# A last tile in two halves ahead of each norm, and a new order of the first loads and of the last norm

## The reference

```python
for l in range(DEPTH):                                   # block one, twice
    x = x + 0.5 * swiglu_ffn(rms_norm(x, ffn1_norm[l]), ffn1_w_in[l], ffn1_w_out[l])
    h = rms_norm(x, mix_norm[l])
    ...                                                  # gMLP, latent attention, SSD; three sigmoid gates
    x = x + merged @ w_out[l]
    x = x + 0.5 * swiglu_ffn(rms_norm(x, ffn2_norm[l]), ffn2_w_in[l], ffn2_w_out[l])
for i in range(DEPTH):                                   # block two: retention, then neighbourhood attention
    h = gated_residual(h, ml, 0, swiglu(ada_in(h, norm_g[i, 0], ml, 0), ffn_w_in[i, 0], ffn_w_out[i, 0]), 0.5)
    h = gated_residual(h, ml, 1, mixer(ada_in(h, norm_g[i, 1], ml, 1)), 1.0)
    h = gated_residual(h, ml, 2, swiglu(ada_in(h, norm_g[i, 2], ml, 2), ffn_w_in[i, 1], ffn_w_out[i, 1]), 0.5)
return rms_norm_2(h, final_norm_g)

def rms_norm(x, gain):
    return x * lax.rsqrt(jnp.mean(x * x, axis=-1, keepdims=True) + EPS) * gain
```

## Time and profile before

| what | value |
|---|---|
| median of three runs | 3204.93 us (3204.53 to 3206.68) |
| time of the profiled execution | 3203.71 us |
| its span, first to last instruction | 3201.80 us |
| TensorE busy, matmuls | 3140.3 us, 98% |
| VectorE, ScalarE, GpSimd busy | 1992.3, 1357.8, 129.9 us |
| mean granted clock of TensorE | 0.997 |
| instructions | 39778 |

### The profile page before, as it was taken

One profiled execution on the slowest core, in us unless ns is written; L12 is line 12 of the kernel. 1 busy time (PEld: TensorE's weight loads), 2 busy tenths in 40 slices (PEclk: granted clock), 3 DMA queues, 4 the chain that ended last, 5 costly groups with the idle time before them and its releaser, 6 DMA issues.

```text
span 3201.8 us, 39778 instructions
## 1 busy us (share of the span) xinstructions
PE 3140.3 (98%) x15550; PEld 2619.4 (82%) x15550; DVE 1992.3 (62%) x2797; ACT 1357.8 (42%) x1907; POOL 129.9 (4%) x160
## 2 busy tenths in 40 slices
PE   8999999999999999999999999999999999999998
PEld 7888888888888887888878888788887788887787
DVE  7968778788687787663344444776335643345665
ACT  6546655455566555323233333322223322245553
POOL 1000000000000000000000000300000000021000
PEclk9999999999999999999999999999999999999999
DMA  8765356677554576542332222254324633253354
GB/s 252 250 193 178 127 197 224 223 236 242 157 184 132 197 246 207 188 147 93 105 99 80 79 93 86 99 171 156 108 92 158 212 117 105 93 139 92 106 189 153
DMA packets 334901, 496.78 MB, mean 155 GB/s; under 512 B 11042, under 2 KB 221884, under 8 KB 334716
## 3 DMA queue, kind: packets, MB, share of 16 engines
q1 hardware_dynamic: 330652, 483.46, 45.5%
q0 software_dynamic: 4064, 10.77, 1.6%
HBM read 493.09 MB, written 1.10 MB: 154 GB/s over the span
## 4 chain that ended last, share of the span: by engine, by line
PE 94%; DVE 3%; issue 1%; ACT 1%; DMA 0%; POOL 0%; SPq 0%; DVEq 0%; POOLq 0%; ACTq 0%
PE bank L587 24%; PE bank L589 23%; PE bank L588 23%; PE bank L643 13%; PE bank L647 7%; PE bank L602 1%; DVE wlo L1750 0%; PE bank L788 0%; PE bank L773 0%; PE bank L1067 0%; DMA raw<-in_w_in_dram 0%; DVE bank L2592 0%; POOL small L2660 0%; PE bank L610 0%; ACT npr L1698 0%
## 5 line engine op out<-in xcount | busy, mean ns | idle before, releaser
L1750 DVE TENSOR_TENSOR wlo<-raw,whi 128x1024 fp32r<-128x1024 f32 (+1 forms) x780 | 939.6, 1213 | 893.7 <-ACT whi L1231 891.6
L1231 ACT ACTIVATE whi<-raw 128x1024 fp32r<-128x1024 f32 (+1 forms) x780 | 815.9, 1050 | 1150.3 <-PE bank L589 990.3
L587 PE MATMUL bank<-xTh,whi 128*128 128x512 f32 (+1 forms) x1312 | 508.2, 387 | 7.2 <-DVE xTl L1835 7.2
L589 PE MATMUL bank<-xTh,wlo 128*128 128x512 f32 (+1 forms) x1312 | 504.0, 384 | 0.0
L588 PE MATMUL bank<-xTl,whi 128*128 128x512 f32 (+1 forms) x1312 | 503.7, 384 | 0.0
L643 PE MATMUL bank<-xT,whi 128*128 128x512 f32 x1760 | 441.5, 393 | 0.9 <-DVE xT L1835 0.5
L587 PE MATMUL bank<-whi,hh 128*128 128x512 f32 x968 | 377.9, 390 | 0.0
L589 PE MATMUL bank<-whi,hl 128*128 128x512 f32 x968 | 376.8, 389 | 0.0
L588 PE MATMUL bank<-wlo,hh 128*128 128x512 f32 x968 | 376.6, 389 | 0.0
L643 PEld LDWEIGHTS bank<-xT,whi 128*128 128x128 f32 x1760 | 316.5, 189 | 63.0 <-issue 3.4
L587 PEld LDWEIGHTS bank<-xTh,whi 128*128 128x128 f32 x1312 | 246.6, 188 | 66.9 <-issue 16.3
(11 more groups left out here) (383 smaller groups left out, 3651.9 us busy)
## 6 DMA issues: line engine op xcount, KB each, us to landing
raw<-in_ffn_w_in_dram SPq DMA_DIRECT2D x176, 1024.0 KB, 5.2
raw<-in_ffn_w_out_dram SPq DMA_DIRECT2D x80, 1024.0 KB, 5.1
mraw<-in_w_mod_dram SPq DMA_DIRECT2D x72, 1024.0 KB, 5.1
raw<-in_w_in_dram SPq DMA_DIRECT2D x44, 1024.0 KB, 5.2
raw<-in_ret_w_in_dram SPq DMA_DIRECT2D x24, 1024.0 KB, 5.1
raw<-in_w_branch_dram SPq DMA_DIRECT2D x12, 1024.0 KB, 5.0
raw<-in_nat_w_qkv_dram SPq DMA_DIRECT2D x12, 1024.0 KB, 5.2
raw<-in_ffn_w_out_dram SPq DMA_DIRECT2D x16, 512.0 KB, 3.4
```

What stands on the lines that cost most here:

```text
L587: pe.matmul(ps, lh, rh, start=start, stop=False, skip_group_check=True)
L589: return pe.matmul(ps, ll, rh, start=False, stop=stop, skip_group_check=True)
L1231: nc.scalar.activation(hi, src, ACT.Copy).then_inc(*e.inc("hi", key, part))
L1750: nc.vector.tensor_tensor(lo, src, hi.bitcast(F32), ALU.subtract).then_inc(*e.inc("lo", key, part))
```

## The change

Seven edits. (1) `rows_by_tile` multiplies the last tile, in the closing slabs, 256 columns at a time: the first half in the tile's own bank, the second from its first closing k on in a bank of its own; `rows` adds three pieces: first, begun (what the own bank had of the second half), rest. This holds for all norms but f1 of layer 0 and g2 of layer 1; behind retention the whole last slab is in halves, with two pieces. (2) The last tile's square of columns 512 to 767 is ScalarE's, that of 768 to 1023 VectorE's, with the sum so far as its start, straight into GpSimd's power. The scaling of the tile before stands between the first piece and the begun one. (3) g2 of layer 0: all squares on ScalarE, scalings one tile later. g2 of layer 1: tile 0 scaled by ScalarE alone. (4) Transposes: tile-by-tile groups for all norms, k by k in the second half, a new order of banks. (5) With 512 rows, half of the low part of the next slab's second part is made ahead of the last scaling. (6) Opening: X in two loads, the identity alone ahead of the slabs, the other constants behind slab 2, the seven norm loads issued by ScalarE, the eight others by GpSimd ahead of its first power; the first part's high rounding on VectorE, its low part behind the turned X, the second part's high rounding between the third and fourth of ScalarE's turned X. (7) End: X times `fg` before the power, scaled afterwards by VectorE (640 columns) and ScalarE (384), four stores.

```diff
-PAIRS, DOWNS, TURNS, MODS, PARAMS = (0, 1, 2, 3, 4, 5), (2, 3, 4, 5), (0, 1, 2, 3, 6, 7, 4, 5), (6, 7), (6, 7, 4)
+PAIRS, DOWNS, TURNS, MODS, PARAMS = (0, 1, 2, 3, 4, 5), (2, 3, 4, 5), (0, 1, 6, 7, 3, 4, 5, 2), (6, 7), (6, 7, 4)
+REST_OF = {"downs": "rest_down", "short": "rest_short", "all": "all"}
...
+def halved(name):
+    return name not in (("f1", 0), ("g2", 1))
+
+def squared_on_act(name, t):
+    return t % 2 == 1 or name == ("g2", 0)
+
+def pieces_of_rows(name, t, n, whole=False):
+    if n == 0 or t != last_tile(name) or not halved(name):
+        return [Piece(n)]
+    first = Piece(n, ("first",), (), 0, 256, True, whole)
+    begun = [] if whole else [Piece(n, ("begun",), (), 256, 256, False, True, True)]
+    return [first, *begun, Piece(n, ("rest",), ("rest",), 0, 256, after_first=whole)]
...
+    if (name, t) == (("g2", 1), 0):
+        return (("act", 0, 512), ("act", 512, 512))
...
-            sp.dma_start(X[:, 0:2, :], w["x"][0].rearrange("(t p) n -> p t n", p=P))\
-              .then_inc(L.sem("x_landed"), 16)
-            sp.dma_start(cst[:, :], consts["cst"][:, 0:C_FLIP]).then_inc(L.sem("gains_landed"), 16)
-            slab_range(0, 1)
-            loads = list(row_loads())
-            for dst, src in loads[:GAIN_LOADS]:
-                sp.dma_start(dst, src).then_inc(L.sem("gains_landed"), 16)
...
+            for t in range(2):
+                sp.dma_start(X[:, t, :], w["x"][0, t * P:(t + 1) * P, :]).then_inc(L.sem(f"x{t}_landed"), 16)
...
+            sp.dma_start(cst[:, 0:P], consts["cst"][:, 0:P]).then_inc(L.sem("ident_landed"), 16)
+            slab_range(0, NRAW)
+            sp.dma_start(cst[:, P:C_FLIP], consts["cst"][:, P:C_FLIP]).then_inc(L.sem("cst_landed"), 16)
...
             for t in range(2):
-                sp.wait_ge(*e.at("out_row", t))
-                sp.dma_start(out[0, t * P:(t + 1) * P, :], fo[:, t, :]).then_inc(L.sem("out_written"), 16)
+                for i, c in enumerate(OUT):
+                    sp.wait_ge(*e.at("out_row", t, i))
+                    sp.dma_start(out[0, t * P:(t + 1) * P, c], fo[:, t, c]).then_inc(L.sem("out_written"), 16)
...
+                    if halved and t == tiles[-1]:
+                        columns(t, ps[t][:, 0:256], slice(0, 256), ("first",), k0, 0, False)
+                        rest = new(*name, t, "rest", ring=REST_OF[ring])
+                        columns(t, rest[:, 0:256], slice(256, 512), ("rest",), k0, k0, True)
+                    else:
+                        columns(t, ps[t][:, :], slice(0, 512), (), k0, 0, t == tiles[-1])
...
-                    groups = (order[:-1], order[-1:]) if name in BEHIND_DOWN else (order,)
+                    groups = (order,) if name == ("f1", 0) else (order[:-1], order[-1:])
...
+                        steps = [(t, k) for t in tiles for k in ks] if half == 0 else [(t, k) for k in ks for t in tiles]
...
+                if not halved(name):
+                    scaled(order[-2])
+                squares(name, order[-1], 1)
+                if halved(name):
+                    scaled(order[-2])
+                first_slab(until, name)
+                scaled(order[-1])
...
+                        if name == ("f1", 0) and k == 2:
+                            first_slab(until, name)
...
+            for dst, src in itertools.islice(row_loads(), GAIN_LOADS):
+                act.dma_start(dst, src).then_inc(L.sem("gains_landed"), 16)
...
+            def low_begun(key, part):
+                src, hi, lo = part_views(key, part)
+                dve.wait_ge(*e.at("hi", key, part))
+                nc.vector.tensor_tensor(lo[:, 0:4, :], src[:, 0:4, :], hi[:, 0:4, :].bitcast(F32), ALU.subtract)
+                half_low.add((key, part))
...
+            def mean_begun(name, t):
+                dve.wait_ge(*e.at("ssa", name, t, 1))
+                link(STT(small[:, t:t + 1], small[:, t:t + 1], EPS, small[:, 4 + t:5 + t], ALU.add, ALU.add))
...
+                if halved(name) and t == last_tile(name):
+                    dve.wait_ge(*e.at("X", name, t, 1, "rest"))
+                    a = X[:, t, 768:1024]
+                    V.tensor_tensor_reduce(junk_v[:, 0:256], a, a, 1.0 / D, small[:, t:t + 1], ALU.mult, ALU.add,
+                                           small[:, 12 + t:13 + t]).then_inc(*e.inc("ms", name, t))
+                    return
...
+                if late:
+                    scaled(order[-3])
+                rows(last, 1, after_first, lambda: mean_begun(name, last))
+                mean_square(name, last)
+                if late:
+                    scaled(before)
+                if T == 512:
+                    low_begun(FIRST[name], 1)
+                scaled(last)
...
-                L.freed[(part, name, g, 0)] = L.events[(stage, name, g)]
+                for mc in range(2):
+                    L.freed[(part, name, g, mc)] = L.events[(stage, name, g)]
...
+                    for p in pieces_of_rows(nxt, t, n):
+                        hooks(p, after_first, before_rest)
+                        if p.waits:
+                            dve.wait_ge(*e.at("down", name, n, t, *p.key))
+                        if p.bank:
+                            dve.wait_ge(*e.at("X", nxt, t, n, "begun"))
+                        x, of = X[:, t, p.x], ("down", name, n, t, *p.bank)
+                        ps, frees = unit(*of)[:, p.ps], of if p.frees else None
+                        if not whos:
+                            STT(x, ps, 0.5, x, ALU.mult, ALU.add).then_inc(*e.inc("X", nxt, t, n, *p.key, frees=frees))
...
+            def before_rest():
+                mean_begun(nm, 1)
+                by_gain(1, slice(512, 768))
+                out_row(0)
+
+            dve.wait_ge(L.sem("fg_landed"), 16)
+            rows(0)
+            squares(nm, 0, 1)
+            mean_square(nm, 0)
+            by_gain(0, slice(0, D)).then_inc(*e.inc("by_gain", 0))
+            by_gain(1, slice(0, 512))
+            rows(1, 1, lambda: None, before_rest)
+            mean_square(nm, 1)
+            by_gain(1, slice(768, D)).then_inc(*e.inc("by_gain", 1))
+            out_row(1)
...
+            loads = list(row_loads())[GAIN_LOADS:]
+            for dst, src in loads:
+                pool.dma_start(dst, src).then_inc(L.sem("params_landed"), 16)
```

More of the change, by code:

```diff
@@ L1 @@
+import itertools
 from contextlib import ExitStack
@@ L722, in rows_by, with rows_by_tile, columns @@
                 return k0
[L724 to L730, removed]
-                    k = k0
+            def rows_by_tile(keys, name, ps, xh, xl, k0, total, ring="all", ahead_of_tile=lambda t: None, halved=False):
+                def columns(t, dst, c, key_of, k, clears, uses):
                     for key in keys:
@@ L1033, in mixers @@
                 wo = {}
+                L.units["short"] = 0
                 for n in range(2):
@@ L1803, in scaled @@
                                 .then_inc(*e.inc("xn", name, t, i))
-                order, scales = tile_order(name, T), []
-                for t in order:
+                order = tile_order(name, T)
+                if name == ("f1", 0):
+                    squares(name, 0, 1)
+                    for t in range(2):
+                        mean_square(name, t)
+                    columns(0)
+                    for t in range(2):
+                        scaled(t)
+                    key = slabs.items[0][0]
+                    src, hi, _ = part_views(key, 0)
+                    dve.wait_ge(*arrival(key))
+                    V.tensor_copy(hi, src).then_inc(*e.inc("hi", key, 0))
+                    dve.wait_ge(*e.at("cols_copied", 0))
+                    return
@@ L1807, in norm @@
+                late = name == ("g2", 0)
+                for i, t in enumerate(order[:-1]):
                     if name == ("g1", 0) and t == 2:
                         dve.wait_ge(*e.at("used", (("f2", 1), "down", 1, 3), 1))
-                    if scales and name in BEHIND_DOWN:
-                        scaled(scales.pop())
-                    if rows and t < tiles:
+                    if late:
+                        if i >= 2:
+                            scaled(order[i - 2])
                         rows(t)
-                    if t % 2 == 0 and t < tiles:
-                        squares(name, t, 1)
-                        mean_square(name, t)
@@ L1816, in norm @@
[L1816 to L1821 removed]
+                        if i:
+                            mean_square(name, order[i - 1])
+                        continue
+                    if i:
+                        before = order[i - 1]
+                        if squared_on_act(name, before) and (name, before) != (("g1", 0), 3):
+                            mean_square(name, before)
+                        scaled(before)
@@ new lines, in norm, with after_first @@
+                    if t < tiles:
+                        rows(t)
+                        if not squared_on_act(name, t):
+                            squares(name, t, 1)
```

(9 more changed lines are left out.)

236 lines of the change are left out of this document (133 added, 103 removed).

## The result

The changed kernel takes 3216.44 us (median of 6 runs, 3215.65 to 3217.65) against 3205.80 for the kernel before beside it: ratio 1.0033, 95% interval 1.0023 to 1.0043. Forecast were 3200.9 us, 0.9987. So it is slower by 10.6 us, outside my range and on the other side. The profiled execution took 3216.15 us with a span of 3214.3; the spans differ by 12.5 us (3201.8 before).

What follows compares the result with a forecast made beforehand. TensorE, busy 98% of the span, bounds the kernel; only its idle time was for sale. Terms -1.6+1.8-0.7-0.1-1.3+0.2-2.0-0.3=-4.0 us take the profiled 3203.71 to 3199.7, forecast as a median of 3200.9; range 3196.0 to 3205.5.

Steps and rivals of the forecast that it cites:

- The order of banks: Transposes' banks: the new order costs nothing, as banks come round two units of 2.8 us later at the least.
- Ungated: Three norms behind a down projection: shorter chain behind the last tile's second half, gain 0.55 us each, -1.6 together.
- rival C: Halved tiles: a half costs VectorE 0.73 us, as a whole does; sum +9.1, 3214.0 us; chance 0.08.
- Projections: Two norms behind the output projections: VectorE is late, the rest queues behind a wait for GpSimd; +1.8 us for both.
- Behind retention: Norm g2 of layer 0: five squares moved from late VectorE to idle ScalarE; -1.3 us (0 to -2.5).
- The half conversion: Low parts, ahead of the last scaling: fits the power's wait of 0.65 us; 0.1 at most where it runs over.
- The three gated norms: r, g1 of layer 1 and n: last turn at 1641.77 against 1642.00; -0.7 us for three.
- Opening: Row loads issued earlier by ScalarE land at 7.3 us, transposes of X start some 3.0 sooner; net -2.0 (+0.3 to -3.2).
- rival A: Opening: small loads keep their 5.3 us landing, so the opening gives 0.2; sum -2.2, 3202.7 us; chance 0.15.
- A's sign: Opening: a transpose of X only after 10.5 us would mean that small loads still take 5.3 us to land.
- End: Tail behind the last matmul: last store issued at 3198.6 as today, with a smaller transfer; -0.3 us (+0.2 to -0.9).
- I put no term for it: Falls of TensorE's clock to half, about half of 3.4 us each: no term, only ±1.7 us in the range.

Runs made afterwards that it cites:

- no_reset: The changed kernel with the ring of short banks no longer set back to 0 ahead of the output projections; 3202.28 us, ratio to before 0.9991.
- low_plain: no_reset with ScalarE's high conversion ahead of its two squares at the output projections, and without the half conversion of the low part; 3200.31 us, 0.9980.
- slab_first: no_reset with GpSimd's eight parameter loads issued behind the two powers of the first norm; 3204.51 us, ratio 0.9996.
- squares_back: no_reset with VectorE squaring the even tiles again at the norm behind retention, as in the kernel before; 3208.74 us, ratio 1.0008.

## Why the prediction was wrong, point by point

- **"The order of banks ... cost nothing: those banks come round again two units of 2.8 us later at the least."** This is the step that failed. I had looked at the new order of the transposes' banks and not at the resets of the rings: two lines, `L.units["downs"] = 0` and `L.units["short"] = 0`, which the shortened diff and the seven edits above leave out and the kernel has. The question for a ring is who still holds the bank at its first place. Here it was the product just made, and VectorE reads it 2.3 and 3.7 us later, behind conversions. With 2.5 us of half clock behind each, the term is +14.3 instead of 0. The reset of the downs' ring costs nothing anywhere on the curve.
- **The norms.** Ungated -0.40, -0.42, -0.44 for -0.53, with the turn 2.1 us behind the second half at the first norm, forecast 2.0; a half costs VectorE 0.42+0.03, as taken from the earlier trace rows, so rival C is out. Projections +0.93 for +0.9, and the turn 3.5 behind the last matmul, as forecast. Behind retention the next matmul came 8.1 us behind its last, forecast 8. I had -1.8 at the full clock and -0.2 at half of it and took a value between; measured were -1.49 in the changed kernel, which stayed at the full clock, and +0.3 in no_reset, which was at half clock for 6.8 us like all three traces with the old code there. How much of the 1.49 is the change and how much the clock can't be told.
- **"The half conversion ... fits the power's wait of 0.65 us; where it runs over, 0.1 at most."** Wrong in mechanism: it fits VectorE's wait, but lengthens GpSimd's work by 0.38. The three gated norms gave -0.37 together for -0.7, and low_plain gets -1.5.
- **Opening: rival A was right.** The last row load took 5.86 us to land (6.4 in no_reset and 7.0 in low_plain, with the same code), for the 3 that I took, and X was turned at 10.93, past the 10.5 given as A's sign. The chain of waits of the changed kernel:

```profile
3.62 0.03 issue
3.65 5.86 DMA rowt<-in_ssd_norm_dram
9.50 0.14 issue
```

  The rule of the Trainium skill ("DMA: Bandwidth & Descriptors", "Issuing engines are not separate DMA queues"), that issuing from another engine saves only the sequencer's time, holds here: 5.32 and 5.86. I also had the first slab 0.7 us sooner; it came 1.0 later, most of it by the eight parameter loads beside it, as slab_first shows (10.10 with them late); that the second slab, issued earlier, makes up the rest is not shown. And the kernel before had the earlier rise of the clock in the execution I read.
- **End.** VectorE came to the rest 2.37 us behind the last matmul, forecast 2.5. The sum is +0.1 for -0.3: the halves cost 0.2, the power took 0.67 beside a product of 256 columns.
- **The clock.** "I put no term for it" was right for the norms and wrong as a habit: I had the cost of one fall (1.7 at most; a stretch of 3.4 us cost 0.7 to 1.6 by what work it fell on, the 6.8 us behind a bank wait 2.5) and did not ask which new wait would be long enough to bring one. The upper end of my range, 3205.5, was said to be A with a fall more; by my own numbers that is 3202.7+1.7=3204.4.

## What to carry to other kernels

Where a ring of buffers is reset or reordered, write down for its first places who holds them, when that reader is done, and what stands in front of it in its own queue; an ordering that looks like bookkeeping can be a wait of microseconds. Compare two traces by the work done (columns), not by the time: the curve showed steps of 0.1 us where medians moved by 2 us with stretches at half clock. And before filling an engine's wait with other work, look whether that work slows the engine it is waiting for.

## What the runs showed that I had not expected

- GpSimd's power (one column of 128 rows) takes 0.55 us alone, and 0.56 beside VectorE's add that reads one operand from a bank; beside a VectorE operation with both operands in SBUF it takes 0.67 (256 columns, end of the changed kernel), 0.93 (512) and 1.47 (product of 1024 columns). The Trainium skill has this rule ("SBUF — State Buffer", "Who interferes with whom": a VectorE instruction with two SBUF inputs contends with a GpSimd instruction that reads SBUF); the traces agree, and I had not looked it up for this edit.
- Executions differ by where TensorE's clock is at its lower level: in the profiled ones, one for each kernel, the first rise came between 14.06 and 18.05 us, and later stretches of 3.4 or 6.8 us came mostly behind idle stretches of norms, two to eight of them, not always the same ones. no_reset's eleven executions lie between 3200.21 and 3206.74 us, with mean granted clocks from 0.998 down to 0.995. The wait of 3.23 us brought none, the five of 4.55 us in three kernels brought 6.8 us each.
- The medians of before and low_plain lie 6.6 us apart where the two profiled spans differ by 3.3 (3201.8 and 3198.5). The mean granted clock goes with the difference: before's profiled execution, at a mean granted clock of 0.997, was one of its better ones; of the 21 executions beside low_plain 14 were at 0.995, 6 at 0.996 and 1 at 0.997, while low_plain had 0.998 or 0.999 in 6 of 11 and 0.996 in 4. At 0.996 the means are 3204.98 and 3202.04: low_plain is 2.9 us faster at the same mean clock, and the rest goes with the clock. squares_back (0.995) and no_reset (0.997) differ in the same way. That the shorter waits are the reason for the higher clock is likely and not shown.
